# Three blocks of a transformer on one core: split f32r products for z, v, output and mix projections, transposes of scaled rows, merges in pieces

## What is computed

```python
for l in range(DEPTH):                       # first block, layers 0 and 1
    h = rms_norm(x, norm1_g[l])
    z = h @ w_in[l]                          # all inputs of the three mixers, and the gates
    (cq, ckv, kpe, gq, gk, gv, glr, gr, su, gates) = split_in(z)
    o_a = mla_mixer(cq, ckv, kpe, ...)       # attention
    o_b = gla_mixer(gq, gk, gv, glr, gr, ...)
    o_c = s5_mixer(su, ...)                  # states by lam_bar = exp(lam * step): scans over time
    g = jax.nn.sigmoid(gates + gate_b[l]).reshape(B, L, 3, D)
    merged = g0 * (o_a @ w_br_mla[l]) + g1 * (o_b @ w_br_gla[l]) + g2 * (o_c @ w_br_s5[l])
    x = x + merged @ w_out[l]
    h2 = rms_norm(x, norm2_g[l])
    x = x + jnp.square(jax.nn.relu(h2 @ w_ff1[l])) @ w_ff2[l]
# second block: pre norm, GLU + convolution mixer and dilated attention, each gated, summed,
# @ w_mix_out, post norm, added to x; then a SwiGLU FFN (w_ffn_in, w_ffn_out) in the same way
```

## Time and profile before

| | us |
|---|---|
| median of 3 runs | 1725.0 |
| the three runs | 1723.35, 1725.0, 1732.68 |
| the profiled execution | 1729.36 |
| its span, first to last instruction | 1727.6 |
| PE busy | 1582.6 (92%) |
| DVE busy | 883.8 (51%) |
| ACT busy | 565.1 (33%) |
| POOL busy | 649.7 (38%) |

### The profile page before, as it was taken

The page is one execution under the profiler, slowest core; times in us unless marked ns, Lnnn a source line. Parts: engine busy times, 40 slices in busy tenths (PEclk is TensorE's granted clock), DMA queues, the critical chain, the costliest instruction groups (busy, mean ns, idle before and its releaser), DMA issues.

```text
span 1727.6 us, 22054 instructions
## 1 busy us (share of the span) xinstructions
PE 1582.6 (92%) x9087; PEld 1339.7 (78%) x9087; DVE 883.8 (51%) x1329; ACT 565.1 (33%) x848; POOL 649.7 (38%) x266
## 2 busy tenths in 40 slices
PE   5998889889999999889888989998999999979997
PEld 4886667557898788667666578897999988579996
DVE  2879522523434567981343225643897533155554
ACT  2110251224444311115113233444544542054443
POOL 0000000004988500000000268895888430059985
PEclk9999997899999999989798989998999999999999
DMA  5543332235666465333232456763666332446663
GB/s 139 131 130 102 101 86 62 73 93 155 194 185 188 127 153 137 98 82 107 59 98 73 147 149 205 233 189 112 193 184 193 112 110 86 127 132 191 186 190 113
DMA packets 331676, 234.35 MB, mean 136 GB/s; under 512 B 20222, under 2 KB 315545, under 8 KB 331576
## 3 DMA queue, kind: packets, MB, share of 16 engines
q1 hardware_dynamic: 331576, 232.94, 46.8%
HBM read 231.82 MB, written 1.09 MB: 135 GB/s over the span
## 4 chain that ended last, share of the span: by engine, by line
PE 77%; DVE 14%; ACT 3%; issue 3%; SPq 1%; POOL 1%; DMA 1%; DVEq 0%; POOLq 0%; ACTq 0%
PE ps L1806 19%; PE ps L580 12%; DVE WK L1443 7%; PE ps L934 5%; PE ps L935 5%; PE ps L936 5%; PE ps L1789 4%; PE ps L1790 3%; PE ps L1791 3%; PE ps L2098 3%; PE ps L951 2%; DVE WK L1584 2%; PE ps L1831 2%; PE ps L1071 1%; PE ps L568 1%
## 5 line engine op out<-in xcount | busy, mean ns | idle before, releaser
L1184 POOL TENSOR_TENSOR w_lo<-raw,w_hi 128x1024 fp32r<-128x1024 f32 x128 | 320.6, 2524 | 849.4 <-ACT w_hi L1218 846.4
L642 POOL TENSOR_TENSOR w_lo<-raw,w_hi 128x1024 fp32r<-128x1024 f32 x134 | 329.0, 2471 | 211.1 <-ACT w_hi L664 201.2
L1806 PE MATMUL ps<-hN,raw 128*128 128x256 f32 (+1 forms) x1376 | 315.3, 391 | 5.0 <-DMA raw<-in_w_in_dram 5.0
L1806 PEld LDWEIGHTS ps<-hN,raw 128*128 128x128 f32 (+1 forms) x1376 | 267.3, 196 | 53.3 <-issue 9.6
L934 PE MATMUL ps<-h_hi,w_hi 128*128 128x256 f32 x800 | 226.2, 283 | 6.2 <-POOL w_lo L642 5.6
L935 PE MATMUL ps<-h_lo,w_hi 128*128 128x256 f32 x800 | 224.6, 281 | 0.0
L936 PE MATMUL ps<-h_hi,w_lo 128*128 128x256 f32 x800 | 224.3, 280 | 0.0
L1218 ACT ACTIVATE w_hi<-raw 128x1024 fp32r<-128x1024 f32 x128 | 135.8, 1061 | 240.5 <-DMA raw<-in_w_ff_dram 162.4
L664 ACT ACTIVATE w_hi<-raw 128x1024 fp32r<-128x1024 f32 x134 | 141.0, 1059 | 151.1 <-DMA raw<-in_w_ffn_in_dram 68.4
L934 PEld LDWEIGHTS ps<-h_hi,w_hi 128*128 128x128 f32 x800 | 151.3, 189 | 7.5 <-issue 7.0
L1789 PE MATMUL ps<-h_hi,w_hi 128*128 128x256 f32 x512 | 145.2, 284 | 8.7 <-POOL w_lo L1184 7.6
(11 more groups left out here) (278 smaller groups left out, 2407.8 us busy)
## 6 DMA issues: line engine op xcount, KB each, us to landing
raw<-in_w_in_dram SPq DMA_DIRECT2D x160, 512.0 KB, 3.8
raw<-in_w_ff_dram SPq DMA_DIRECT2D x128, 512.0 KB, 4.1
raw<-in_w_ffn_in_dram SPq DMA_DIRECT2D x44, 512.0 KB, 3.9
raw<-in_w_ffn_out_dram SPq DMA_DIRECT2D x22, 512.0 KB, 3.6
raw<-in_w_out_dram SPq DMA_DIRECT2D x16, 512.0 KB, 3.5
raw<-in_w_br_s_dram SPq DMA_DIRECT2D x8, 512.0 KB, 3.5
raw<-in_w_br_gla_dram SPq DMA_DIRECT2D x8, 512.0 KB, 3.5
raw<-in_w_br_mla_dram SPq DMA_DIRECT2D x8, 512.0 KB, 3.4
```

The lines of the kernel that those rows point to most:

```text
L642: nc.gpsimd.tensor_tensor(out=w_lo[i % RING][:, 0:kt * n], in0=raw[i % RING][:, 0:kt * n], in1=w_hi[i % RING][:, 0:kt * n], op=ALU.subtrac ...
L1184: nc.gpsimd.tensor_tensor(out=w_lo[i % RING][:, 0:kt * n], in0=raw[i % RING][:, 0:kt * n], in1=w_hi[i % RING][:, 0:kt * n], op=ALU.subtract)\
L1806: last = MM(out, w[:, k, c0:c0 + n], x[:, x0 + k, :], start=k == 0, stop=k == kt - 1)
```

## The change

- The z and v slabs get a name of their own, `w_in_z`, and are split (SPLIT), as are w_out and, in the second block, w_mix_out. 23 + 8 slabs in each layer and 8 in the second block are rounded by ACT and get their remainder from POOL. The gates and the other small weights stay f32. z and v use h_hi and h_lo, so that DVE writes both h_lo and hN at the start of a layer.
- `x_to_h` transposes rows that DVE has scaled (`norm_scale`, two instructions of 512 columns for each block of tokens) instead of multiplying by a diagonal. `norm_rows` squares 512 columns at a time, adds the first sum to eps with an Identity and uses this as the bias of Ln. At the start of a layer the first token block goes ahead of the small vectors.
- `merge` works in four pieces of 512 columns, each behind its own slab of the branch. For the last merge ACT rounds each piece into h_hi (`merged_hi`) and DVE writes h_lo (`merged_piece`). PE's output and mix projections go through `by_rows`, three matmuls of 512 columns for each f32 one.
- ACT rounds the first two slabs of a layer and of the second block (`prep(2)`) before it writes h_hi.
- The 17 small DMAs of `second_tables` become nine behind I_FF + 6 (`second_vectors`) and eight behind I_FF + 12; the bias goes behind I_FF + 17.

The diff, cut to its core:

```diff
+    s = [("w_in_z", 0, KD, c, n) for c, n in Z_COLS]
+    s += [("w_in_z", 4 * P * (i % 2), 4, C_GV + 256 * (i // 2), 256) for i in range(4)]
...
-SPLIT = ("w_ff1", "w_ff2")
-SPLIT2 = ("w_in", "w_ffn_in", "w_ffn_out")
+SPLIT = ("w_in_z", "w_out", "w_ff1", "w_ff2")
+SPLIT2 = ("w_in", "w_mix_out", "w_ffn_in", "w_ffn_out")
...
+        def norm_rows(act, A_, l, k, b, ready):
+            n = 2 * (2 * k + b)
+            c = [nt[:, 2 * n + i:2 * n + i + 1] for i in range(4)]
+            act.wait_ge(*ready(2 * b))
+            A_(tok(sqt, 2 * b), tok(xt, 2 * b), ACT.Square, accum_out=c[0]).then_inc(norm_sq.s, 1)
+            act.wait_ge(norm_sq.s, norm_sq(l, n + 1))
+            A_(c[1], c[0], ACT.Identity, scale=1.0 / DM, bias=C("eps")).then_inc(norm_ln.s, 1)
+            act.wait_ge(*ready(2 * b + 1))
+            A_(tok(sqt, 2 * b + 1), tok(xt, 2 * b + 1), ACT.Square, accum_out=c[2]).then_inc(norm_sq.s, 1)
+            act.wait_ge(norm_sq.s, norm_sq(l, n + 2))
+            act.wait_ge(norm_ln.s, norm_ln(l, n + 1))
+            A_(c[3], c[2], ACT.Ln, scale=1.0 / DM, bias=c[1]).then_inc(norm_ln.s, 1)
+            act.wait_ge(norm_ln.s, norm_ln(l, n + 2))
+            A_(c[3], c[3], ACT.Exp, scale=-0.5).then_inc(norm_rs.s, 1)
+
+        def norm_scale(dve, V, l, k, b):
+            c = 4 * (2 * k + b) + 3
+            dve.wait_ge(norm_rs.s, norm_rs(l, 2 * k + b + 1))
+            for i in (2 * b, 2 * b + 1):
+                V.tensor_scalar(tok(sqt, i), tok(xt, i), nt[:, c:c + 1], None, ALU.mult).then_inc(xs_ok.s, 1)
...
+        def x_to_h(pe, l, k, b):
+            for j in range(KD):
+                if j % 4 == 0:
+                    pe.wait_ge(xs_ok.s, xs_ok(l, 4 * k + 2 * b + j // 4 + 1))
+                last = nc.tensor.transpose(PAall[:, T * j + P * b:T * j + P * b + P], sqt[:, b, P * j:P * j + P],
+                                           C("ident"))
...
+        def merged_hi(act, A_, l, at, src, p):
+            act.wait_ge(hf_ok.s, hf_ok(l, at + p + 1))
+            A_(piece(h_hi, p), piece(src, p), ACT.Copy).then_inc(mh_ok.s, 1)
+
+        def merged_piece(dve, tt, l, g, other, p):
+            tt(piece(g, p), piece(g, p), piece(other, p), ALU.add).then_inc(hf_ok.s, 1)
+            dve.wait_ge(mh_ok.s, mh_ok(l, p + 1))
+            tt(piece(h_lo, p), piece(g, p), piece(h_hi, p), ALU.subtract).then_inc(ml_ok.s, 1)
...
             pre_norm(1)
             act.wait_ge(cols2_ok.s, 4)
+            prep(2)
             h_rounded(0, "g_pre_mix")
...
             take_pair(3)
+            for p in range(NP):
+                merged_hi(act, A_, L, NP, G2, p)
+                prep(J_MO + p + 1)
             prep(J_FF + 1)
...
-                            second_tables(sp)
-                    if i == I_FF + 8 and l == DEPTH - 1:
+                            second_vectors(sp)
+                    if i == I_FF + 12 and l == DEPTH - 1:
+                        second_tables(sp)
+                    if i == I_FF + 17 and l == DEPTH - 1:
...
+                norm_rows(act, A_, l, 0, 0, x_ready)
                 act.wait_ge(vec_in.s, vec_in(l, vec_in.per))
                 A_(dtr[:, 0:2], dtr[:, 0:2], ACT.Exp).then_inc(dt_row.s, 1)
+                norm_rows(act, A_, l, 0, 1, x_ready)
+                prep(2)
+                act.wait_ge(cols_ok.s, cols_ok(l, 1))
+                h_rounded(0, "norm1_g")
...
+                for p in range(NP):
+                    merged_hi(act, A_, l, NP, G, p)
+                    prep(I_OUT + p + 1)
                 prep(I_FF + 1)
...
-                norm_diag(dve, V, l, 0)
+                norm_scale(dve, V, l, 0, 1)
+                norm_lo(dve, stt, l, col, "norm1_g")
                 norm_h(dve, V, l, col, "norm1_g")
...
                 def merge(k):
+                    for p in range(NP):
+                        dve.wait_ge(used.s, used(l, (I_BRA, I_BRB, I_BRC)[k] + p + 1))
+                        stt(piece(g, p), piece(g, p), 1.0, ps_piece(p), ALU.add, ALU.mult).then_inc(mg_ok.s, 1)
+                        dve.wait_ge(mg_ok.s, mg_ok(l, NP * (2 - k) + p + 1))
...
-                    product32(l, i, out, 0, n, hN, fresh=None if t else 0).then_inc(used.s, 1)
+                    product(l, i, out, 0, n, h_hi, h_lo, fresh=None if t else 0).then_inc(used.s, 1)
...
                 for k in range(KD):
-                    w, _ = weights(l, I_OUT + k)
+                    w = weights(l, I_OUT + k)
+                    if k == 0:
+                        pe.wait_ge(mg_ok.s, mg_ok(l, 3 * NP))
                     if k % 2 == 0:
-                        pe.wait_ge(hf_ok.s, hf_ok(l, NP + k // 2 + 1))
...
+                        pe.wait_ge(ml_ok.s, ml_ok(l, k // 2 + 1))
+                    by_rows(MM, l, w, h_hi, h_lo, k, k == 0, k == KD - 1)
```

More of the change, by code:

```diff
@@ L341, in build @@
         consts_in = sig("consts_in", 0)
-        x_in = sig("x_in", 0)
+        x_in = [sig(f"x_in{b}", 0) for b in range(NT)]
         vec_in = sig("vec_in", 16 * (len(ROWS) + 2))
@@ L561, in norm_lo, with by_rows @@
                     ins.then_inc(hl_ok.s, 1)
[L563 to L571, removed]
+        def x_to_h(pe, l, k, b):
[4 more added lines that the diff above has]
+                                           C("ident"))
+                if b == 1 and j % 2:
+                    last.then_inc(ht_ps.s, 1)
+        def merged_hi(act, A_, l, at, src, p):
[5 more added lines that the diff above has]
+            tt(piece(h_lo, p), piece(g, p), piece(h_hi, p), ALU.subtract).then_inc(ml_ok.s, 1)
         def down(MM, l, w, f, k, first_k, last_k):
+            by_rows(MM, l, w, f_hi[f], f_lo[f], k, first_k, last_k)
+        def by_rows(MM, l, w, f_h, f_l, k, first_k, last_k):
             wh, wl = (x[:, 0, :] for x in w)
@@ L1064, in pe_second @@
                 last.then_inc(used.s, 1)
-            pe.wait_ge(ao_ok.s, 1)
+            pe.wait_ge(mg_ok.s, mg_ok(L, NP))
             for k in range(KD):
-                w, _ = weights(J_MO + k)
+                w = weights(J_MO + k)
                 if k % 2 == 0:
[L1069 to L1075, removed]
-            x_to_h(pe, MM, L, 1)
+                    pe.wait_ge(ml_ok.s, ml_ok(L, k // 2 + 1))
+                by_rows(MM, L, w, h_hi, h_lo, k, k == 0, k == KD - 1)
+            x_to_h(pe, L, 1, 0)
+            x_to_h(pe, L, 1, 1)
             def up(c):
@@ L1401, in _ @@
                 take_pair(3)
-                prep(I_BRA + RING)
                 act.wait_ge(evac.s, evac(l, U_GATE0 + 4))
@@ L1830, in token_major @@
                     for k in range(4):
-                        last = MM(out[:, b, :], hN[:, 4 * half + k, tb], w[:, k, :],
-                                  start=half == 0 and k == 0 and b == 0, stop=half == 1 and k == 3,
-                                  skip_group_check=True)
+                        x, first_k = 4 * half + k, half == 0 and k == 0 and b == 0
+                        MM(out[:, b, :], h_hi[:, x, tb], w[0][:, k, :], start=first_k, stop=False, skip_group_check=True)
+                        MM(out[:, b, :], h_hi[:, x, tb], w[1][:, k, :], start=False, stop=False, skip_group_check=True)
+                        last = MM(out[:, b, :], h_lo[:, x, tb], w[0][:, k, :], start=False,
+                                  stop=half == 1 and k == 3, skip_group_check=True)
                 return last
@@ L2093, in _ @@
                 for k in range(KD):
[L2094 removed]
+                    w = weights(l, I_OUT + k)
+                    if k == 0:
+                        pe.wait_ge(mg_ok.s, mg_ok(l, 3 * NP))
                     if k % 2 == 0:
[L2096 to L2104 removed]
+                        pe.wait_ge(ml_ok.s, ml_ok(l, k // 2 + 1))
+                    by_rows(MM, l, w, h_hi, h_lo, k, k == 0, k == KD - 1)
+                x_to_h(pe, l, 1, 0)
+                x_to_h(pe, l, 1, 1)
                 def up(c):
```

140 lines of the change are left out of this document (59 added, 81 removed).

## The result

| | before | after |
|---|---|---|
| median, us | 1724.2 (4 runs, 1720.6 to 1732.7) | 1761.1 (4 runs, 1760.3 to 1764.3) |
| span of the profiled execution, us | 1727.6 | 1759.5 |
| ratio of the times, 95% interval | | 1.021 (1.017 to 1.025) |

The account below looks back on a forecast made before the run. PE leads before the scans by only 9 and 7 us; DVE's table, held by remainders, would then bound them. Terms 65.6 - 3.2 + 1.6 - 5.0 - 4.9 - 5.5 = +48.6 us gave 1776 us, range 1737 to 1803.

Parts of the forecast that it names:

- z and v slabs: Split z and v slabs in both layers: remainders delay DVE's table build and so the scans; +65.6 us.
- The mechanism: In the sine and cosine table build each POOL remainder holds DVE's next SBUF-only instruction for its full 2.40 us.
- rival 2: Half held: POOL starves in pauses, DVE slips through, remainders cost 1.2 us each; 1737 us, chance 0.08.
- Merges: Merging per 512 columns shortens PE's wait for merge B by 1.6 us a layer; -3.2 us.
- Output projection and norm: Split output projection -0.6 us and the norm behind it +1.4, per layer +0.8; +1.6 us in all.
- the queue described: Ahead of the output projection ACT waits for the first w_out load, DVE for ACT and remainders; start +2.6 us.
- waits hidden: Lower bound of the output projection term, -7 us, if the waits in front of it are hidden.
- Start of the second block: With prep(2) ahead of h_hi, PE starts the second block about 1184.2 instead of 1189.16; -5.0 us.
- Mix projection: Same queue ahead of the mix projection, faster split slabs, sooner post norm and transposes; -4.9 us, bounds -10 to 0.
- Spread tables: Spreading small loads in layer 1's FFN cuts PE's 6.7 us remainder wait; -5.5 us, bounds -6.7 to -3.
- I leave about 1.2 us: What remains of PE's 6.7 us wait in layer 1's FFN after spreading the small loads.
- Rival 3: Dearer: gates inside the scans run at the lower clock, more than 17 remainders meet the table; 1803 us, chance 0.10.

Follow-up runs that it names:

- the three kernels with short or no remainders: Changed kernel with plain f32 z and v slabs, 1701.0 us; with remainders cut to 8 columns from the fourth z slab on, 1685.7; to half their columns, 1721.2.
- with 8 columns: Changed kernel with GpSimd subtracting only the first 8 of 1024 columns per remainder from the fourth z slab on (timing only): 1685.7 us, ratio to before 0.975.
- the new order: Changed kernel with plain z and v slabs and ScalarE rounding each projection slab one merged piece later: 1686.1 us, ratio to before 0.977.
- whole merges: Changed kernel with plain z and v slabs and branches B and C merged in one instruction behind all four slabs: 1708.3 us.

## Why the prediction was right

The side and the range held: 1776 was said, 1737 to 1803, and 1761.1 measured. By its steps:

- **z and v slabs**, +65.6 predicted, +52.3 in the traces. The mechanism is the one described, and the three kernels with short or no remainders show it. The sign in the profile came out too: first scan product released by DVE (at 138.1 us, where 146 was named), PE done with v at 92.8 us and idle from 103.9 on, POOL busy for 40.7 of the 49.4 us from its first remainder in the table to the last of z and v, and of DVE's 48.1 busy us from 40 to 90 only 12.3 work (35.8 are hold), where under 20 was said. Three sizes were off. 17 remainders meet the table, as said, but one costs 2.11 us and not 2.40 (35.8 instead of 40.8). In layer 0 the table starts 2.6 us sooner (37.3 against 39.9), where the start was taken as unmoved: 35.8 - 2.6 - 9.1 = 24.1. In layer 1 the start came 0.6 us sooner against all around it: 35.7 - 0.6 - 6.9 = 28.2. The means of the small instructions, said to be near 1 us, were 0.44 (41 of them up to 96 us), and POOL had seven pauses of 0.6 to 2.4 us, which was named as a sign of rival 2: the short instructions pass in the pauses, up to 11 in one, but one for each remainder is held in full, so the price stands. By the Trainium skill's rule of the exclusive lock ("SBUF — State Buffer", "SBUF: two separate sides") the one that starts first has the shared pair of ports for its whole instruction and the other waits. The traces agree: the hold grows with the remainder's length but for the 0.3 us, and with 8 columns it was POOL that waited, twice for over 0.9 us.
- **Merges**, -3.2 predicted. PE's wait for the merge fell from 4.8 to 1.6 us in the two layers together, exactly that. The step that was mis-sized is what follows the wait: the low clock behind it went as well, 1.7 us a layer, so -6.6. The prediction had counted the clock where a new wait came and not where an old one became shorter. Another 2 us between the scans and the output projection come from single stretches at a lower clock, which no run ties to a part of the change.
- **Output projection and norm**, +1.6 predicted, +2.6 measured (+1.4 and +1.2 a layer). The start came 2.7 us late (2.6 said), by the queue described, behind a wait of 6.15 us. The run took 25.2 us instead of 24.5, at a granted clock of 0.54 over its first 6 us. The bound of -7, "waits hidden", wasn't far off: the new order reached -4.7 of wait and -2 of clock, 6.0 in all in layer 0.
- **Start of the second block**, -5.0 predicted; the shift falls from 43.3 to 38.2 there, -5.1. No run undid prep(2), so its part is read from the timeline alone: PE's first product waits 1.51 us instead of 4.92.
- **Mix projection**, -4.9 predicted; from 38.2 to 33.3, -4.9. Its start is 1.7 us late where 2.9 was said, the other terms a little smaller than said.
- **Spread tables**, -5.5 predicted, -2.9 in the traces (46.2 to 43.3). The step that was off is "I leave about 1.2 us": the wait came back further on, 2.8 us long in the changed kernel. How much the spreading is worth in the whole kernel is not settled (11.0 and 4.3 us between the medians, 0.9 and 2.5 in this part).
- The end of the kernel gained 1.4 us that no term named.

The sum: 52.3 - 8.8 + 2.6 - 2.9 - 5.1 - 4.9 - 1.4 = +31.8, against +48.6 said. So the mechanism of the large term was right, its sizes were not, and the errors of the small ones partly cancelled. Of the 17 us between them 13.3 are the price of a remainder and the start of the table, 5.6 the merges, 1.4 the end; the table loads (2.6) and the projections (1.0) went the other way. Rival 3 (gates inside the scans at the lower clock) added nothing: from first to last scan instruction of layer 0 both kernels take 67.4 us, though PE's clock is 0.71 in the window of the scans.

## What to carry to other kernels

Before a product is moved to cheaper matmuls, ask which engine pays for the operand: here 0.67 us of PE per slab cost 2.1 us of a DVE that had 7 to 9 us of slack, once in a stage where all of its work lies in SBUF. Keep POOL's two-input instructions out of such stages, or shorten them: the hold grows with their length. And in an engine's program put nothing that others need behind a wait for a load: moving the roundings back by one place in front of three projections gave 15 us.

## What the runs showed of the hardware

- A GpSimd subtraction of two SBUF operands held VectorE's two-input SBUF instruction for its own length less 0.3 us (0.96 of 1.29, 2.11 of 2.39 us), and at 8 columns (0.20 us) not at all. One VectorE instruction is held by each of several subtractions in a row. The other way round, two subtractions of 8 columns lasted 1.11 and 1.16 us behind VectorE instructions of 1.23 us. Of instructions with one SBUF input the reciprocal passed inside a remainder (0.25 us); of seven 128 x 16 scalings of sm (L1609) the shortest took 0.17 and the longest 2.32 us, so these are held too.
- The granted clock over the 6 us behind a wait of PE was 0.54 behind 6.2 us (output projection), 0.72 behind 2.4 us (rotation, whole merges), and 1.00 at the same places behind 1.5 and 0.8 us. 0.54 lies next to the 1.2 GHz level, 1.00 is 2.4 GHz, and 0.72 is a mean of both: two products of 512 columns follow each other in 0.86 us at the lower level and in 0.47 at the upper. At these places a shortened wait gave back more than itself. It is no rule of the wait's length: of three waits of 3.27 us in the kernel before, two were followed by 1.00 and one by 0.72.
